# Second feed-forward: the up projections of two of its parts formed from seven half-size products each, and weight sums that take one operand from a PSUM bank

## What is computed

```python
def swiglu(x, w_gate, w_up, w_down):
    return (jax.nn.silu(x @ w_gate) * (x @ w_up)) @ w_down
...
x = layer_norm(ALPHA * x + 0.5 * swiglu(x, ffn2_w_gate, ffn2_w_up, ffn2_w_down), ln3_g, ln3_b)
```

## Time and profile before

| | us |
|---|---|
| median of 3 runs | 2619.48 |
| lowest, highest | 2616.82, 2621.07 |
| the profiled execution | 2619.98 |
| its span in the trace | 2618.1 |
| PE busy | 2572.8 (98%) |
| DVE, POOL, ACT busy | 1371.5, 1178.9, 856.1 |

### The profile page before, as it was taken

One profiled execution on the slowest core, in us unless ns is written; L12 is line 12 of the kernel. 1 busy time (PEld: TensorE's weight loads), 2 busy tenths in 40 slices (PEclk: granted clock), 3 DMA queues, 4 the chain that ended last, 5 costly groups with the idle time before them and its releaser, 6 DMA issues.

```text
span 2618.1 us, 50175 instructions
## 1 busy us (share of the span) xinstructions
PE 2572.8 (98%) x20164; PEld 2431.5 (93%) x20164; DVE 1371.5 (52%) x2363; ACT 856.1 (33%) x1482; POOL 1178.9 (45%) x628
## 2 busy tenths in 40 slices
PE   9999999999999999999999999999999999999997
PEld 9999999998899999999999999999977788888887
DVE  6665444964443473424466654439644535834246
ACT  3222224235532242323252222242355322523232
POOL 4444435412244455646454444355132454657562
PEclk9999999999999999999999999999999999999998
DMA  5333324302223323332233333243122333332322
GB/s 162 97 91 89 89 81 106 81 23 63 58 77 96 97 76 111 97 97 81 81 108 96 91 88 90 81 103 81 27 63 59 85 90 102 97 113 85 109 73 73
DMA packets 457372, 226.92 MB, mean 87 GB/s; under 512 B 42384, under 2 KB 456336, under 8 KB 457200
## 3 DMA queue, kind: packets, MB, share of 16 engines
q1 hardware_dynamic: 450880, 217.09, 29.6%
q10 hardware_dynamic: 6320, 7.41, 1.0%
HBM read 220.20 MB, written 2.10 MB: 85 GB/s over the span
## 4 chain that ended last, share of the span: by engine, by line
PE 86%; DVE 7%; issue 3%; ACT 2%; POOL 1%; DMA 1%; ACTq 0%; SPq 0%; POOLq 0%; DVEq 0%
PE ps L675 65%; PE ps L810 8%; PE ps L785 4%; PE ps L698 3%; PE ps L1014 1%; PE ps L1099 1%; POOL w_lo L590 1%; PE ps L1138 1%; PE ps L1114 1%; PE ps L1103 1%; PE ps L1021 1%; DVE stat L2063 1%; DVE s_back L2102 1%; DMA w_raw<-in_ffn_w_gate 1%; DVE s_state L2092 1%
## 5 line engine op out<-in xcount | busy, mean ns | idle before, releaser
L590 POOL TENSOR_TENSOR w_lo<-w_raw,w_hi 128x1024 fp32r<-128x1024 f32 (+4 forms) x432 | 937.7, 2178 | 1207.6 <-ACT w_hi L1257 1206.3
L1257 ACT ACTIVATE w_hi<-w_raw 128x1024 fp32r<-128x1024 f32 (+4 forms) x432 | 406.5, 945 | 697.4 <-PE ps L675 459.7
L675 PE MATMUL ps<-x_hi,w_hi 128*128 128x264 f32 (+2 forms) x3104 | 461.6, 299 | 6.2 <-ACT hid_rest L1257 3.6
L675 PE MATMUL ps<-x_hi,w_lo 128*128 128x264 f32 (+2 forms) x3104 | 454.3, 296 | 0.9 <-POOL w_lo L590 0.9
L675 PE MATMUL ps<-x_lo,w_hi 128*128 128x264 f32 (+2 forms) x3104 | 454.1, 296 | 0.0
L675 PEld LDWEIGHTS ps<-x_hi,w_hi 128*128 128x128 f32 x3104 | 410.5, 188 | 26.1 <-ACT hid_rest L1257 4.0
L675 PEld LDWEIGHTS ps<-x_hi,w_lo 128*128 128x128 f32 x3104 | 411.3, 188 | 17.1 <-POOL w_lo L590 1.7
L675 PEld LDWEIGHTS ps<-x_lo,w_hi 128*128 128x128 f32 x3104 | 411.3, 188 | 15.4
L1796 DVE TENSOR_TENSOR ps<-hid_rest,ps 128x528 f32<-128x528 f32 (+1 forms) x88 | 62.3, 708 | 319.4 <-PE ps L675 307.6
L675 PE MATMUL ps<-hid_hi,w_hi 128*128 128x264 f32 (+1 forms) x1008 | 155.2, 301 | 0.1
L675 PE MATMUL ps<-hid_hi,w_lo 128*128 128x264 f32 (+1 forms) x1008 | 153.7, 299 | 0.0
(11 more groups left out here) (335 smaller groups left out, 3891.8 us busy)
## 6 DMA issues: line engine op xcount, KB each, us to landing
w_raw<-in_ffn_w_up SPq DMA_DIRECT2D x88, 512.0 KB, 3.7
w_raw<-in_w_in SPq DMA_DIRECT2D x82, 512.0 KB, 3.7
w_raw<-in_ffn_w_down SPq DMA_DIRECT2D x64, 512.0 KB, 3.5
w_raw<-in_ffn_w_gate SPq DMA_DIRECT2D x48, 512.0 KB, 3.8
w_pair<-in_ffn_w_gate SPq DMA_DIRECT2D x40, 512.0 KB, 5.2
w_raw<-in_ffn_w_down SPq DMA_DIRECT2D x32, 384.0 KB, 3.1
w_raw<-in_w_o SPq DMA_DIRECT2D x16, 512.0 KB, 3.6
w_raw<-in_conv_w_out SPq DMA_DIRECT2D x16, 256.0 KB, 2.7
```

Source lines behind the costliest of these rows:

```text
L590: pool.tensor_tensor(held(w_lo, c), src, held(w_hi, c).bitcast(f32), ALU.subtract).then_inc(w_split, 1)
L675: ins = nc.tensor.matmul(dst, wk, x[:, k0 + k, tokens], start=first and k == 0 and n == 0, stop=last and k == n_tiles - 1 and n == 2)
L1257: return nc.scalar.activation(out, in_, f, **kw)
```

## The change

In parts 1 and 2 of the second feed-forward (eight pairs in each layer) the up projections of a pair are crossed as the gates were. The gates of a pair are now one unit (forms in banks 0 to 3), the ups another (banks 4 to 7); part 0 keeps its plain ups. A unit is named (part, pair, 0 for gates or 1 for ups).

- SP loads pairs of up weights in `w_pair` too, each buffer again once the splits of the unit before last are done; `w_raw` carries only down weights in these parts.
- `add_weights` makes four sums for every unit. Units of odd number put three of them in other memory (`k_rope`, `stat`), so that two sets are held. In all units of parts 1 and 2 but the first of each part, one operand of each sum is read out of PSUM, where ACT has copied a block of `w_pair` (`copy_block`, three copies of 128x512 a unit, in banks 1, 3 and 2 of the four in which the coming unit will accumulate).
- DVE's order in the two parts interleaves the coming unit's sums with `combine`'s steps. The hidden work changes: DVE multiplies gate and up (`make_hidden`), ACT rounds the result to `hid_hi` (`round_hidden`), DVE subtracts (`rest_hidden`). For a pair it stands at the start of the next pair.
- The first down product of an iteration now begins with all but the last two hidden tiles, and `layer_norm_first` of this feed-forward stands inside the first down product.

```diff
-        else:
-            GROUP_OF.append((part, q))
-            F2_COLS += [8 * P if k in ups_at(part, q) else 4 * P for k in range(FORMS + 2)]
+        for what in range(2 if part else 1):
+            UNIT_AT[part, q, what] = len(F2_COLS) + (FORMS * what if part else forms_at(part, q))
+            UNITS.append((part, q, what))
+        F2_COLS += ([4 * P] * (2 * FORMS) if part else
+                    [8 * P if k in ups_at(part, q) else 4 * P for k in range(FORMS + 2)])
...
+BESIDE = [n for n, (part, q, what) in enumerate(UNITS) if part and (q or what)]
...
+        beside = [kr[:, 0:HALF_SLOT], *(stat[:, k, 0:HALF_SLOT] for k in (3, 4))]
...
+            return [w_sum[:, 0], *(beside if g % 2 else (w_sum[:, k] for k in range(1, 4)))]
...
+            return ps[:, 4 * (g % 2) + (1, 3, 2)[k], 0:HALF_SLOT]
...
+                pe.wait_ge(*free[0])
                 pe.wait_ge(turned_ready, l * 4 + 1)
                 form(0, 1, turned(0), True)
                 form(1, 0, own(low, first), True)
...
+                pe.wait_ge(*free[1])
+                pe.wait_ge(sum_made, 4 * g + 3)
                 pe.wait_ge(turned_ready, l * 4 + 2)
                 form(2, 3, turned(1), True)
+                pe.wait_ge(sum_made, 4 * g + 4)
                 pe.wait_ge(turned_ready, l * 4 + 3)
                 form(3, 2, turned(2), True)
...
+                if part:
+                    crossed(l, (part, q, 1), 4, ((hid_done, a + 1), (hid_done, a + 2)))
+                else:
+                    up(0)
+                    up(1)
...
-                            product(pair(d % 2, sp), c, 0, gh, gl, nf - 1, True, False, sp=sp)
+                            product(pair(d % 2, sp), c, 0, gh, gl, nf - 2, True, False, sp=sp)
+                            pe.wait_ge(hid_done, n0 + (nf + 1))
+                            if shift:
+                                layer_norm_first(l, 2)
+                            product(pair(d % 2, sp), c, nf - 2, gh, gl, 1, False, False, at=nf - 2, sp=sp)
...
+                    if what == 0:
+                        if q:
+                            round_hidden(part, 2 * q - 2)
+                        keep()
+                    copy_block(n + 1, 0)
+                    round_at(l, c)
+                    copy_block(n + 1, 1)
+                    round_at(l, c + 1)
+                    if what:
+                        keep()
+                    round_at(l, c + 2)
+                    copy_block(n + 1, 2)
+                    for k in range(3, FORMS):
+                        round_at(l, c + k)
...
+                        if q:
+                            make_hidden(part, f - 2)
+                            rest_hidden(part, f - 2)
+                        add_weights(m + 1, (0,))
+                        combine(gate, (0,))
+                        add_weights(m + 1, (1,))
+                        combine(gate, (1, 2))
+                        add_weights(m + 1, (2,))
+                        combine(gate, (3,))
+                        add_weights(m + 1, (3,))
+                        combine(gate, (4,))
```

More of the change, by code:

```diff
@@ L528, in ffn_crossed @@
                             continue
-                        group += 1
-                        if group < N_CROSS:
-                            load_pair(group)
-                        for j in range(2):
+                        for what in range(2 if part else 1):
+                            n = UNITS.index((part, q, what))
+                            if n + 1 < N_CROSS:
+                                load_pair(n + 1)
+                        for j in range(0 if part else 2):
                             load(l, c + ups_at(part, q)[j], 0, 8 * P, rows(wu, l, 0, KD, (f0 + 2 * q + j) * P, P), KD)
@@ L792, in last_tiles, with crossed @@
                             spread_root(n, 0)
-            def crossed(l, part, q, a, t0):
-                c, g, sp = B_FFN2 + GROUPS_AT[part, q], l * N_CROSS + GROUP_OF.index((part, q)), stream(l)
+            def crossed(l, unit, banks, free):
+                c, g, sp = B_FFN2 + UNIT_AT[unit], l * N_CROSS + UNITS.index(unit), stream(l)
                 first, second = sp.halves
@@ L809, in form @@
                         for k in range(KD // 2):
-                            ins = nc.tensor.matmul(ps[:, bank, 0:sp.half], held(w, c + n, k * P, (k + 1) * P), x[:, k],
+                            ins = nc.tensor.matmul(ps[:, banks + bank, 0:sp.half], held(w, c + n, k * P, (k + 1) * P), x[:, k],
                                                    start=start and i == 0 and k == 0,
@@ L1421, in round_turned, with round_hidden, copy_block @@
                          scale=-1.0 if n == 1 else 1.0).then_inc(turned_hi_done, 1)
+                def round_hidden(part, f):
+                    for j in range(2):
+                        act.wait_ge(hid_made, l * (NF - PARTS[0][1]) + PARTS[part][0] - PARTS[0][1] + (f + j + 1))
+                        ACTV(two(gh[:, f + j, sp.all]), apart(2 + j, sp)).then_inc(hid_rounded, 1)
+                def copy_block(n, k):
+                    g = l * N_CROSS + n
+                    if n not in BESIDE:
+                        return
+                    part, q, what = UNITS[n]
+                    if k == 0:
+                        act.wait_ge(pair_loaded[g % 2], (g // 2 + 1) * 32)
+                        done = (l * 2 + 1) * NF + PARTS[part][0] + 2 * q + 2
+                        act.wait_ge(*((hid_done, done) if what else (silu_done, done)))
+                    j, h = ((1, 0), (0, 0), (0, 1))[k]
+                    ACTV(copy_bank(g, k), w_pair[:, g % 2, j, h * HALF_SLOT:(h + 1) * HALF_SLOT]).then_inc(block_copied, 1)
@@ L1862, in hidden, with combine, make_hidden, rest_hidden @@
                     split_hidden(f, pair(up, sp), sp, st)
-                def combine(g, c):
-                    bank = lambda k: ps[:, k, 0:sp.half]
+                def combine(at_, steps=range(5)):
+                    c, g, what = b0 + UNIT_AT[at_], l * N_CROSS + UNITS.index(at_), at_[2]
+                    bank = lambda k: ps[:, 4 * what + k, 0:sp.half]
                     own, u2, u3 = (v[:, 0:sp.half] for v in (kept, *part_sum))
                     dve.wait_ge(first_kept, g + 1)
-                    for k, (out, a, b, form) in enumerate(((u2, own, bank(3), 2), (u3, u2, bank(2), 3),
-                                                           (bank(3), u3, bank(1), 3), (bank(2), u2, bank(2), 5),
-                                                           (bank(1), u2, bank(1), 6))):
+                    for k in steps:
+                        out, a, b, form = ((u2, own, bank(3), 2), (u3, u2, bank(2), 3), (bank(3), u3, bank(1), 3),
+                                           (bank(2), u2, bank(2), 5), (bank(1), u2, bank(1), 6))[k]
                         dve.wait_ge(chunk_done, done_at(l, c + form))
                         follow(tt(out, a, b, ADD), crossed_step, 5 * g + (k + 1))
+                def make_hidden(part, f):
+                    n0 = PARTS[part][0] + f
+                    for j in range(2):
+                        dve.wait_ge(silu_done, (l * 2 + 1) * NF + n0 + (j + 3))
+                        up = apart(2 + j, sp)
+                        stt(up, up, (1.0, -1.0)[j], two(glf[:, f + j, sp.all]), MUL, MUL).then_inc(hid_made, 1)
+                def rest_hidden(part, f):
+                    n0 = PARTS[part][0] - PARTS[0][1] + f
+                    for j in range(2):
+                        dve.wait_ge(hid_rounded, l * (NF - PARTS[0][1]) + n0 + (j + 1))
+                        tt(two(gl[:, f + j, sp.all]), apart(2 + j, sp), two(ghf[:, f + j, sp.all]), SUB).then_inc(hid_done, 1)
                 for part, (f0, nf) in enumerate(PARTS):
```

171 lines of the change are left out of this document (104 added, 67 removed).

## The result

The changed kernel takes 2603.53 us (median of five runs, 2599.50 to 2604.46), the kernel before 2619.48: a ratio of 0.9936, with an interval of 0.9921 to 0.9950. The profiled execution took 2604.27 us, its span 2602.5. The forecast was 2606.0 with a range of 2598.0 to 2613.5; the time lies in the range and the direction was right.

The account below looks back on a forecast made before the run. PE alone was taken to bound the changed stretches. 21.0 us saved on PE less 7.4 us of new waits gave 13.6 us less than before, a forecast of 2606.0 us with a range of 2598.0 to 2613.5.

Parts of the forecast that it names:

- What PE loses: Crossed ups save PE 1.41 us a pair in layer 0 and 1.22 in layer 1, 21.0 us in all.
- POOL: In each pair, 14 subtractions take POOL 17.9 us, within PE's 20.4 or 19.8; PSUM operands cost POOL nothing.
- The waits before form 5: Gate units: step 1 of `combine` comes late, PE waits 0.60 us (layer 1) or 0.50 (layer 0); 7.4 us lost.
- The up units: Form 4 of the up units needs `crossed_first`, ready at 5.41 us, due at 5.66: no wait, 0.2 us spare.
- Loads: `w_pair` loads land 2 us or more ahead of ACT's copies, narrowest in a part's third unit; all covered.
- The end of a part: First down product's 4.2 us cover `rest_hidden` (2.94, 3.54); layer norm's first take ends at 11.0, wanted at 11.4.
- No new wait: Rival: ACT's and DVE's queues run 0.6 us faster, form 5 never waits, all 21.0 us stay: 2598.5; chance 0.20.
- Longer waits: Rival: each link costs 0.04 us more, sixteen gate units lose 0.5 us more each: about 2612; chance 0.13.
- PSUM operand of no help: Rival: sums with a PSUM operand still contend with POOL, 1.0 us more per gate unit: about 2622; chance 0.04.
- The clock falls: Rival: each of the 16 new waits is followed by a fall of PE's clock, 27 us lost: 2633; chance 0.05.

Follow-up runs that it names:

- the version without waits: Changed kernel with step 1 before the second sum and, in a part's first gate unit, form 6 rounded first: 2594.19 us, ratio 0.9902.

## Why the prediction came out

**What PE loses: right.** 21.0 us forecast. A unit takes 10.19 and 9.93 us in the second place too, and the version without waits is 20.9 us shorter over the stretch. Of the changed kernel's 13.1 us, this is the whole credit.

**POOL: right, and the copies are needed.** Subtractions at 1.295 to 1.30 us throughout, DVE's sums at 0.687, ACT's copies at 0.59. A pair's fourteen subtractions fit. POOL was busy for 82% of the pairs of part 1 (67.71 of 83.00 us), not the forecast 90%. What failed is the price of a sum from SBUF alone. I divided 0.96 us by four sums, but POOL was idle until 2354.30, when two of the four were done: 0.96 belongs to two, 0.48 each. Over all sums of the run without copies it is 0.34 to 0.42 us, since some still meet an idle POOL. With 0.24 the case without copies came to 19.8 us a pair, which just fits; with 0.34 it is 17.9 + 8 x 0.34 = 20.6 us, more than the 19.8 to 20.4 that a pair has.

The Trainium skill, page SBUF — State Buffer, section Who interferes with whom, has an exclusive lock: whoever starts first keeps the other out for its whole instruction. I read it as a charge on POOL alone, 0.69 us a sum. The trace agrees that there is a price for two SBUF inputs and none for one, and also that either engine can be the one kept out. Timelines of POOL and DVE, kernel before, layer 0:

```profile
1122.51 2.88 POOL L590 TENSOR_TENSOR w_lo<-w_raw,w_hi 128x1024 fp32r<-128x1024 f32 x1 [2.22 <-ACT w_hi L1257]
```

```profile
1123.16 2.77 DVE L1856 TENSOR_TENSOR w_sum<-w_pair 128x512 f32<-128x512 f32 x1
```

The sum began 0.65 us after POOL's subtraction and ended 0.54 us behind its end (1125.39), after 2.77 us where it takes 0.69 alone. In the rows shown such a sum cost POOL some 0.5 us, or DVE 1.0 and 2.1.

**The waits before form 5: right in place, cause and size.** Forecast 0.60 and 0.50, in the first of a part 0.25 and 0.16; measured by the length of the units 0.54 and 0.45, and 0.34 and 0.22. Step 1 began at 7.03 instead of 7.12, PE at 7.55 instead of 7.68. Two of the sixteen are longer by some 0.35: the first of part 2 in layer 0 and the fourth of part 1 in layer 1, in which DVE starts nearly 0.4 later behind its releaser than elsewhere. They recur in the same places in the other runs of this order; why is open. The sum is 7.7 us against 7.4.

**The up units: right.** No wait before form 4 in any of them, with the 0.2 us of room.

**Loads: right for PE, and too kindly worked out.** No load held PE in the changed kernel. But the "up to 5.2 us of flight" was the median; the earlier trace rows has 7.7 as the longest. ACT waited 0.16 us for the third unit's load already, and once the waits before form 5 were gone 0.69. And the down blocks were not there 2 us ahead: ACT stood 5.84 us before one at the end of layer 1's last part, where the work behind it still had room.

**The end of a part: right in outcome, with a premise that did not hold.** Layer norm's first take ends at 11.0 as forecast, before 11.4. But `hid_lo` was done 0.8 us later than worked out, because of that down block; there was room for it, and it is used up in the version without waits (0.3 us late in layer 1).

**What the sum missed.** 13.1 us of the 15.95 between the medians lie in the stretch. The forecast has no term for the other 2.9; without them the time would be 2619.5 - 13.1 = 2606.4, closer to the forecast than what was measured. They lie in code that the change leaves as it was: in the profiled executions, the idle end of the program aside, the granted clock was at its lower level for 23.8 us before and 20.4 after, away from the pairs, at half the work 1.7 us. It differs from run to run (13.6 us in the second profile of the changed kernel). The mean granted clock over all its runs is about 0.9955 against 0.9936 for the kernel before. Why unchanged code has fewer of these falls is not settled.

**The rivals.** *No new wait*: did not occur, but the version with step 1 moved is that case, at 2596 and 2594 where 2598.5 was worked out. *Longer waits* and *PSUM operand of no help*: refuted by the rows above. (*Longer waits* was headed 2612, but its own 8 us on 2606 make 2614.) *The clock falls*: no wait of 0.2 to 0.9 us in the pairs had a fall behind it, nor one of the 0.9 to 1.5 us in the run with the copy made twice; their stretches stand at 1.00. Behind some longer waits there was one: after the 3.6 us in the run with sums from SBUF (the unit from 2403.52) the clock is at 0.57 over four microseconds, the lower level (1.2 GHz) for most of them:

```profile
2413.00:2417.00 4.00, 4.00 (x21) 4.00 (x22) 1.27 (x3) 1.06 (x1) 4.00 (x2) 0.57 0.09 26
```

The Trainium skill's section "A second HAM failure mode: psum-queue depth-cycling" (page TensorE: Matmul & The Clock Gate) tells of frequent short idles that make the clock oscillate; this trace does not show that for sixteen waits, some 20 us apart.

## What to carry to other kernels

When an engine gets a new duty, write out the queue of each engine that takes part with start times, and look for a step that is queued behind the new duty without needing it: here one step moved in DVE's order (step 1 ahead of a sum) gave 7 us more on top of the change's 16. In these runs an engine at 95% of its time (POOL) did not show itself as a wait on each unit; it used up the slack of buffers and loads, and the wait stood at the end of the part, on other engines' names. To see what bounds there, compare busy shares, not only the releasers. And follow such a wait past the stretch that you changed: 7 of the 17 us that the copies are worth lie in the down products behind it.
